# An encoder layer's opening: gate columns and first weight slab loaded earlier, early half worked off in quarters

## The reference, cut to what matters

```
h = _rmsnorm(x, norm_mix)
proj = h @ w_in                       # w_in: 2048 x (3*1024 + 4)
q, k, v = ...                         # 1024 columns each
f_logit = proj[..., 3 * A:] + b_f     # the last four columns: the gate
cum = cumsum(log_sigmoid(f_logit))
logits = q k^T / sqrt(d) + cum_t - cum_s
x = x + softmax(logits) v @ w_out
x = x + (silu(h' @ w_gate) * (h' @ w_up)) @ w_down
return _rmsnorm(x, final_norm)
```

## Time and profile before

| | |
|---|---|
| Median of 3 runs | 1697.6 us (1697.36 to 1698.68) |
| The profiled execution | 1697.54 us, its span 1695.7 us |
| TensorE (PE) busy | 1682.6 us, 99% of the span |
| VectorE (DVE) busy | 1337.2 us, 79% |
| ScalarE (ACT) busy | 853.8 us, 50% |
| GpSimd (POOL) busy | 210.6 us, 12% |

### The profile page before, as it was taken

The page is one execution under the profiler, slowest core; times in us unless marked ns, Lnnn a source line. Parts: engine busy times, 40 slices in busy tenths (PEclk is TensorE's granted clock), DMA queues, the critical chain, the costliest instruction groups (busy, mean ns, idle before and its releaser), DMA issues.

```text
span 1695.7 us, 25155 instructions
## 1 busy us (share of the span) xinstructions
PE 1682.6 (99%) x8977; PEld 1449.5 (85%) x8977; DVE 1337.2 (79%) x1485; ACT 853.8 (50%) x1075; POOL 210.6 (12%) x327
## 2 busy tenths in 40 slices
PE   9999999999999999999999999999999999999998
PEld 7888888888888888888888888888888888888886
DVE  6888778968877777777777777777789978878886
ACT  6454555444445454445454445454455444444454
POOL 1010102001011111111111111111100001000043
PEclk9999999999999999999999999999999999999999
DMA  8746667942277777776777776777788886867854
GB/s 236 168 100 162 149 150 218 316 100 74 73 208 180 186 186 186 195 187 174 186 181 204 195 195 177 186 187 185 197 241 244 251 240 194 253 178 192 257 156 146
DMA packets 311630, 317.55 MB, mean 187 GB/s; under 512 B 10256, under 2 KB 259360, under 8 KB 305168
## 3 DMA queue, kind: packets, MB, share of 16 engines
q1 hardware_dynamic: 291968, 231.79, 44.2%
q0 software_dynamic: 19152, 83.37, 25.0%
q10 hardware_dynamic: 448, 1.55, 0.3%
HBM read 205.83 MB, written 30.41 MB: 139 GB/s over the span
## 4 chain that ended last, share of the span: by engine, by line
PE 74%; DVE 1%; issue 0%; ACT 0%; POOL 0%; POOLq 0%; ACTq 0%; DVEq 0%
PE ps L3075 31%; PE ps L3126 23%; PE ps L3081 16%; PE ps L3059 2%; PE ps L3064 1%; PE ps L3041 1%; DVE split L2540 0%; DVE down_slot L2553 0%; PE ps L3045 0%; ACT split L1726 0%; DVE tmp L1907 0%; PE ps L2737 0%; DVE xres L2569 0%; ACT xres L1607 0%; POOL var L1233 0%
## 5 line engine op out<-in xcount | busy, mean ns | idle before, releaser
L1617 ACT ACTIVATE split<-raw 128x1024 fp32r<-128x1024 f32 x295 | 312.1, 1058 | 342.5 <-DVE raw L2410 112.9
L2399 DVE TENSOR_TENSOR split<-raw,split 128x1024 fp32r<-128x1024 f32 x295 | 360.5, 1223 | 139.1 <-ACT split L1617 135.0
L3126 PE MATMUL ps<-split,operand_hi 128*128 128x512 f32 x1232 | 380.5, 389 | 0.2
L3126 PEld LDWEIGHTS ps<-split,operand_hi 128*128 128x128 f32 x1232 | 231.2, 188 | 49.8 <-ACT split L1726 0.9
L3075 PE MATMUL ps<-hT,split 128*128 128x512 f32 x984 | 246.4, 392 | 0.0
L3126 PE MATMUL ps<-split,operand_lo 128*128 128x512 f32 x616 | 239.7, 389 | 0.0
L1726 ACT ACTIVATE split<-down_slot 128x2048 fp32r<-128x2048 f32 (+1 forms) x82 | 145.6, 1781 | 173.9 <-PE ps L3126 84.8
L3075 PEld LDWEIGHTS ps<-hT,split 128*128 128x128 f32 x984 | 177.0, 189 | 31.7
L2540 DVE TENSOR_TENSOR split<-down_slot,split 128x2048 fp32r<-128x2048 f32 (+1 forms) x84 | 177.2, 2109 | 19.8 <-ACT split L1726 16.2
L3075 PE MATMUL ps<-oT,split 128*128 128x512 f32 x656 | 164.3, 392 | 0.0
L3081 PEld LDWEIGHTS ps<-hT,split 128*128 128x128 f32 x984 | 134.2, 190 | 9.6
(11 more groups left out here) (281 smaller groups left out, 2469.3 us busy)
## 6 DMA issues: line engine op xcount, KB each, us to landing
raw<-in_ffn_w_gate_up_dram SPq DMA_DIRECT2D x172, 512.0 KB, 5.0
raw<-raw POOLq DMA_DIRECT2D x99, 512.0 KB, 4.5
down_slot<-in_ffn_w_down_dram SPq DMA_DIRECT2D x32, 1024.0 KB, 7.1
a_sums<-pack SPq DMA_DIRECT2D x22, 1024.0 KB, 6.4
raw<-in_fox_w_in_dram SPq DMA_DIRECT2D x36, 512.0 KB, 4.7
down_slot<-down_slot POOLq DMA_DIRECT2D x16, 1024.0 KB, 8.1
operand_raw<-a_sums SPq DMA_DIRECT2D x28, 512.0 KB, 7.3
down_slot<-in_ffn_w_down_dram SPq DMA_DIRECT2D x16, 768.0 KB, 6.5
```

Source lines behind the costliest of these rows:

```text
L1617: nc.scalar.activation(ring(r, 0, n), source, ACT.Copy).then_inc(t_hi, 1)
L2399: nc.vector.tensor_tensor(ring(r, 1, n), source, f32(ring(r, 0, n)), ALU.subtract).then_inc(t_lo, 1)
L3126: ins = nc.tensor.matmul(banks[:, tile, :], operand[e][part][:, i, tile * P:(tile + 1) * P], down_ring(dn, part_of_t, e)[:, i * BANK:(i + ...
```

## The change

On SP's queue, slab 0 is loaded in two halves of eight chunks each, both ahead of x tile 2 (it was one transfer behind tile 2); the first half has a semaphore of its own, `slab_first`. The gate's columns are loaded on ScalarE's queue, as its first instruction, instead of behind x tile 1 on SP's. ScalarE waits for them and spreads them before it copies `gain_col`; VectorE subtracts its low parts before its first chunk. Both engines then go through the early half in `QUARTERS` of 6, 4, 4 and 2 chunks, each followed by one piece of slab 0. `square_x(0)` moves from the start of ScalarE's list to behind the early half, and `square_x(1)` from behind `split_hi(At(1))` to the same place, ahead of `take_x(1)`.

TensorE runs three warm-up products instead of two. It goes through the early half by quarters too, gate then product of slab 0, with the turning of tile 2's chunks 0 to 5 and 6 to 9 in the third and fourth. Tile 3's chunks 0 to 9 are turned after the early product (they were turned inside it). The late half alternates: four chunks of the gate, two chunks each of tiles 2 and 3 turned (in the first three rounds), four chunks of the product; before, all turning came first, then the whole gate, then the whole product. The semaphore `warmed` is gone.

```diff
         LOW = 16
+        QUARTERS = (range(0, 6), range(6, 10), range(10, 14), range(14, ND))
...
             load_x(0)
             load_x(1)
-            with nc.allow_non_contiguous_dma(reason="the gate's four columns"):
-                sp.dma_start(wf[:], w_in_v[:, :, 3 * A:3 * A + H]).then_inc(wf_in, 16)
+            sp.dma_start(tile_of(At(0), P)[:, 0:QK8, :], w_in_v[:, 0:QK8, 0:P]).then_inc(slab_first, 16)
+            load(At(0), tile_of(At(0), P)[:, QK8:ND, :], w_in_v[:, QK8:ND, 0:P], first=True)
             load_x(2)
-            load(At(0), tile_of(At(0), P), w_in_v[:, :, 0:P], first=True)
             load_x(3)
...
+            with nc.allow_non_contiguous_dma(reason="the gate's four columns"):
+                act.dma_start(wf[:], w_in_v[:, :, 3 * A:3 * A + H]).then_inc(wf_in, 16)
             act.wait_ge(const_set, 2)
             act.dma_start(gain_rows[0:ND, :], norm_mix.rearrange("a (c p) -> (a c) p", p=P)).then_inc(gain_in, 16)
-            square_x(0)
-            act.wait_ge(gain_turned, 1)
-            nc.scalar.activation(gain_col[:], ps[:, SC[3], 0:ND], ACT.Copy).then_inc(gain_taken, 1)
-            act.wait_ge(gain_taken, 1)
-            take_x(0, range(0, 2))
             act.wait_ge(wf_in, 16)
             act.wait_ge(const_set, CONSTS)
             for r in range(4):
                 nc.scalar.activation(pad[:, :, r::32], wf[:], ACT.Copy).then_inc(pad_hi, 1)
-            take_x(0, range(2, ND))
-            act.wait_ge(raw_in[0], 16)
-            for j in range(4):
+            act.wait_ge(gain_turned, 1)
+            nc.scalar.activation(gain_col[:], ps[:, SC[3], 0:ND], ACT.Copy).then_inc(gain_taken, 1)
+            act.wait_ge(gain_taken, 1)
+            for j, chunks in enumerate(QUARTERS):
+                take_x(0, chunks)
+                if j == 0:
+                    act.wait_ge(slab_first, 16)
+                elif j == 2:
+                    act.wait_ge(raw_in[0], 16)
                 nc.scalar.activation(piece(split[0], j), piece(raw, j),
                                      ACT.Copy).then_inc(first_hi if j < 3 else hi_ready, 1)
+            square_x(0)
+            square_x(1)
             take_x(1)
             split_hi(At(1), first=True)
-            square_x(1)
             square_x(2)
             square_x(3)
...
-            dve.wait_ge(gain_taken, 1)
-            take_x(0, range(0, 2))
             for r in range(4):
                 dve.wait_ge(pad_hi, r + 1)
                 nc.vector.tensor_tensor(pad[:, :, LOW + r::32], wf[:], f32(pad[:, :, r::32]),
                                         ALU.subtract).then_inc(pad_lo, 1)
-            take_x(0, range(2, ND))
-            for j in range(4):
+            dve.wait_ge(gain_taken, 1)
+            for j, chunks in enumerate(QUARTERS):
+                take_x(0, chunks)
...
-            stay_warm(2, SC[3])
+            stay_warm(3, SC[3])
...
-            gate(EARLY, between=(7, 9, 11, 13, 15))
-            for j in range(4):
+            for j, chunks in enumerate(QUARTERS):
+                gate(EARLY, chunks)
+                if j == 2:
+                    turn_x(2, range(0, 6))
+                elif j == 3:
+                    turn_x(2, range(6, 2 * FIVE))
                 pe.wait_ge(first_lo if j < 3 else lo_ready, j + 1 if j < 3 else 1)
                 project(first, PROJ[0], EARLY, range(4 * j, 4 * j + 4), wait=False)
-                if j == 0:
-                    turn_x(3, range(0, 2 * FIVE))
-            for c in range(2 * FIVE, ND, 2):
-                turn_x(2, range(c, c + 2))
-                turn_x(3, range(c, c + 2))
-            gate(LATE).then_inc(f_done, 1)
-            project(first, PROJ[0], LATE).then_inc(slab_used, 1)
+            turn_x(3, range(0, 2 * FIVE))
+            for j in range(4):
+                ins = gate(LATE, range(4 * j, 4 * j + 4))
+                if j < 3:
+                    for tb in (2, 3):
+                        turn_x(tb, range(2 * FIVE + 2 * j, 2 * FIVE + 2 * j + 2))
+                else:
+                    ins.then_inc(f_done, 1)
+                ins = project(first, PROJ[0], LATE, range(4 * j, 4 * j + 4), wait=False)
+            ins.then_inc(slab_used, 1)
```

More of the change, by code:

```diff
@@ L591, in fox_layer @@
         x_in = [sem(f"x_in{i}") for i in range(NT)]
+        slab_first = sem("slab_first")
         gain_in = sem("gain_in")
@@ L628, in fox_layer @@
         pad_lo = sem("pad_lo")
-        warmed = sem("warmed")
         f_done = sem("f_done")
@@ L2892, in stay_warm, with gate @@
                 for _ in range(n):
-                    ins = nc.tensor.matmul(ps[:, bank, :], warm[:, 0:P], warm, start=True, stop=True)
-                ins.then_inc(warmed, 1)
-            def gate(h, between=()):
+                    nc.tensor.matmul(ps[:, bank, :], warm[:, 0:P], warm, start=True, stop=True)
+            def gate(h, chunks):
                 out = ps[:, GATE + h, :].rearrange("p (n t) -> p n t", n=2)
                 pe.wait_ge(x_lo, ND * h + 2)
-                for k in range(ND):
+                for k in chunks:
                     pe.wait_ge(x_lo, ND * h + k + 1)
                     ins = nc.tensor.matmul(out, pad[:, k, :], h_both[:, :, h, k, :], start=k == 0, stop=k == ND - 1)
-                    if k in between:
-                        turn_x(2, range(k - 7, k - 5))
                 return ins
```

## The result

The changed kernel takes 1704.98 us (median of 6 runs, 1704.13 to 1705.77) where the kernel before, run beside it, takes 1697.53 (6 runs, 1697.36 to 1698.68). The ratio is 1.0041 with an interval of 1.0031 to 1.0052: slower, by 7.45 us between the medians. Runs of one and the same kernel fall into two groups about 1.2 to 1.4 us apart (the kernel before near 1697.4 and near 1698.8), so the ratios and the marks in the timelines say more than the plain medians. The forecast was 1700.8 with a range of 1699.2 to 1703.1, so the time lies beyond the range, on the side of rival A. The profiled execution took 1705.77 us.

A forecast was written before the change was run, and what follows sets the result against it. TensorE, busy nearly the whole span, was taken as the bound, so an opening delay stays to the end. 0 + 1.4 + 0.8 + D (1.0) = +3.2 us on 1697.6 gave 1700.8, range 1699.2 to 1703.1.

The forecast's parts named there:

- rival A: Opening: gate columns or gain rows land late, D is 1.9 to 3.3, time 1701.7 to 1703.1; chance 0.30.
- part 5: Start of the kernel: third warm-up product and moved gate columns delay VectorE's first chunk; 1.0 us taken.
- D: How much later VectorE's first chunk comes after the change; taken as 1.0 us, not less than 0.3.
- V: Start of VectorE's first chunk, 9.93 us before the change; the first slab product was forecast at V+3.1.
- Part 1: Early half by quarters: TensorE's early work is done 1.3 us ahead, less D.
- Part 2: Late half: gate(LATE) waits 1.1 us, handing back the whole gain of Part 1; sum 0+D.
- S: Start of turning x tile 3 on TensorE, forecast at V+12.3 = 22.2+D.
- Part 3: Slab 1 comes late through split_hi(1) and split_lo(1): TensorE stalls 1.4 us.
- Part 4: Behind slab 1: TensorE's slab 2 waits 0.8 us more for the q half.
- B: Rival: slab 1 isn't late, only the wait for the late half is real; 1697.9 to 1698.7; chance 0.08.
- C: Rival: only the first stall, before slab 1, is real and the q half is in time; 1700.0; chance 0.10.
- 0.38 for slower: Whole kernel: the chance given to a time slower than 1701.0 us.

The follow-up runs named there:

- e1: The changed kernel with the gate columns on SP's queue ahead of x tile 0, gain rows still on ScalarE's queue: 1701.4 us, ratio 1.0018.
- e3: The kernel before with only the gate columns moved, as first transfer on ScalarE's queue: 1704.89 us, ratio 1.0038.
- e8: The changed kernel itself, run again beside other experiments: 1705.17 us, ratio 1.0041 against the kernel before.
- e2: The changed kernel with two more warm-up products on TensorE after x tile 0 is turned: 1704.52 us, ratio 1.0038 against the kernel before.
- e6: The kernel before with only TensorE's late half written as in the change: 1701.62 us, ratio 1.0023.
- e5: e1 with the late half of the kernel before and square_x(1) back behind split_hi(1), early quarters kept: 1697.74 us, ratio 0.9998 against the kernel before.
- e4: The changed kernel with ScalarE's two transfers swapped, gain rows ahead of the gate columns: 1706.64 us, ratio 1.0053 against the kernel before.

## Why the prediction was wrong

**The step that failed is part 5, D = 1.0** ("the packets cost the same engines' time wherever issued"). D was 5.15. The engines' time was indeed hardly more (12.0% of 11.5 us for ScalarE's queue, 1.4 us, against the 1.1 us taken from the earlier trace rows): what the step left out is the order in which the packets finish. On a second queue most of the 16-byte packets went one for one with packets of SP's queue, so columns issued first of all landed at about 11.8 us and held the gain rows behind them. By 11.5 us the trace has all 2096 packets of ScalarE's queue and 1965 of SP's: both tiles (256 of 8 KB), the first half slab (1024 of 512 B) and two thirds of the second. e1 takes away the second queue alone and D falls to 1.6; e3 puts it in alone and loses the whole 7.4 us. Rival A had the mechanism and both waits (columns ahead of gain_col on ScalarE, gain rows on TensorE), but its price was short: it let the columns land behind the first half slab at 10.8 and left the clock out, which made D 3.3 at most. They landed 1.0 later than that, and ScalarE's first chunk came 2.3 behind them, not 1.5.

, which the prediction gives for rival A, doesn't show this mechanism: its 2 packets are the very first of that transfer, in the last 0.1 us of the row, and from 36.5 to 37 us the count is 57 against 96. A nearer sign in the same trace was the transfer of the gain rows: 32 packets, 8 KB, and 5.2 us from issue to landing beside the tiles, where e1, with the columns on SP's queue, has 2.4.

The Trainium skill, DMA: Bandwidth & Descriptors, section "Queues, rings and completion order", says that each engine alternates between queues packet by packet, with a packet holding many descriptors. The trace agrees on the alternation while both queues have packets, with 74 against 74 and 1170 against 1170; it shows nothing of a turn of many, as one packet of 16 bytes went for one of 8 KB.

**The floor of D was off too.** Part 5 priced the third warm-up product at two records of 0.87, tile 0 turned from 6.5 and D not less than 0.3. Six records took 4.63, and tile 0 was turned at 6.04 (5.79 in e8) against 5.82: 0.2 at most. This changes nothing in the time.

**The clock was not priced.** In the forecast TensorE never stood long. With 4.4 us of idle time the granted clock fell to 0.50. e2 sets the price at 1.3 to 1.4 us in the marks: about 0.7 lies inside D (the first chunk came at 13.41 there and at 14.12 in the changed kernel), 0.7 to 0.8 behind V.

**Part 1 held, but for the clock.** The first slab product started at V+3.9 (forecast V+3.1), since its transposes and gates ran at half the clock. From there to the turning of tile 3 it was 9.1 us (9.2). In e1, at full clock, VectorE's first chunk is at 11.54, the first slab product at V+3.1 (14.64) and the turning of tile 3 at V+12.3 (23.87), both as forecast. Both half slabs were in time.

**Part 2 held.** gate(LATE) came at S+2.2 with a listed wait of 0.97 (forecast 1.1), and the late product ended at S+13.2, its last twelve products from 39.87 at 0.12 each (forecast 13.1). The early half's lead of 1.3 us was handed back, as e6 and e5 show from both sides. The squares were hidden: ScalarE was done with the early half and both squares before 26 us and next needed at 28.55.

**Part 3 held.** Slab 1 waited 1.27 us for split_lo(1), forecast 1.4. **Part 4 held within 0.3:** slab 2 waited 0.51, forecast 0.8, and 0.74 in e6.

**The sum with measured terms.** Slab 1 started at 42.73 instead of 35.38, 7.35 later: 5.15 (D), 0.8 (V to the first product), and 1.4 (the late slab). Another 0.5 stands before slab 2, and 0.1 in the product of slab 1. That is 7.95 of the 8.3 us by which the spans differ; the rest, about 0.35, is spread over the later kernel and was not traced. Between the medians it is 7.45. Part 2 stands in this sum as 0, since the early gain and the late wait cancel.

**The rivals.** The first chunk of ScalarE at 14.12, beyond 10.5, is the prediction's own sign for A. B and C fall: all three waits are there, in the changed kernel and in e6 alone. The chance of 0.38 for slower was too low, and the range ended at A's upper price, which was worked out as if the second queue could delay the columns by one load only.

**Not settled.** Why the kept clock (e2) shows 1.3 to 1.4 us in the marks and only some 0.6 in the medians stays open. The mean clocks of the single runs (under e2) speak for a clock that falls in full in only about half of the runs; repeated runs of one kernel differ by as much as this difference.

## What to carry to other kernels

A transfer of thousands of tiny packets is not first because it is issued first: on a queue of its own its packets go one for one with the neighbour queue's as long as that has any, and its price follows from how large those are. Count its packets, look at what the other queue has in front, and keep it on one queue, at the place where it costs a microsecond or two. Then read what stands in the program behind each engine's wait: here one wait for the columns held the gains, and through them all of TensorE. And when an early product is started sooner, check that the work for the next half still runs under it; otherwise the gain comes back as a wait there and as a late split of the next slab.

## What the runs showed of the hardware

- SP's and ScalarE's queues alternated packet for packet over whole windows: 74 and 74, 1170 and 1170 in the changed kernel, 93 and 93 in e3, whether the neighbour's packets held 8 KB or 512 B. Between two tiles' packets (5 to 5.5 us) the small ones ran ahead, 472 against 32. ScalarE's small packets went at 62 a microsecond in e3 and at 468 in the changed kernel; by themselves, on SP's queue, at 1983.
- A transfer issued behind the columns on the same queue held ScalarE in its issue for 4.82 us, and for 7.35 in e3. In e4, issued first, it took 0.40.
- At the start of the kernel the warm-up products took 0.87 us a record, and 0.77 in the changed kernel, while the granted clock is listed as 1.00 from 0 to 6 us in both; the same products at 7.50 us in e2 took 0.47.
